# Two experts' rows in one V gather, added in pairs on alternate column halves of TensorE

## What is computed

```python
sc, sel = lax.top_k(cand, PEER_TOPK)
idx = jnp.take_along_axis(cidx, sel, axis=-1)
g = jax.nn.softmax(sc, axis=-1)
u_sel = jnp.take(u_tab, idx, axis=0)
hid = jnp.einsum('td,thkd->thk', xb, u_sel).astype(jnp.float32)
a = (g * jax.nn.gelu(hid, approximate=False)).astype(xb.dtype)
return jnp.einsum('thk,thkd->td', a, jnp.take(v_tab, idx, axis=0))
```

## Time and profile before

| | us |
|---|---|
| median of 3 runs | 3440.01 |
| lowest and highest | 3436.83, 3442.25 |
| profiled execution | 3433.54 |
| its span, first to last instruction | 3431.8 |

### The profile page before, as it was taken

The page is one execution under the profiler, slowest core; times in us unless marked ns, Lnnn a source line. Parts: engine busy times, 40 slices in busy tenths (PEclk is TensorE's granted clock), DMA queues, the critical chain, the costliest instruction groups (busy, mean ns, idle before and its releaser), DMA issues.

```text
span 3431.8 us, 27484 instructions
## 1 busy us (share of the span) xinstructions
PE 2676.2 (78%) x7344; PEld 1233.6 (36%) x7344; DVE 2760.4 (80%) x6506; ACT 797.4 (23%) x1426; POOL 2296.1 (67%) x2198
## 2 busy tenths in 40 slices
PE   7567769988777877877878789988878877666777
PEld 4424424554333323444422234453433323222222
DVE  1588896787899998789898987898899989777761
ACT  4104132662111104142010141663101012200012
POOL 0176666666667777667777677777767767677771
PEclk9788979999889988988999889999988998877788
DMA  6599999999999999999999999999999999999993
GB/s 245 204 392 412 403 354 362 337 317 346 331 330 409 402 410 412 413 403 392 409 409 409 389 402 374 407 367 374 409 374 388 404 408 397 412 393 385 391 401 110
DMA packets 330977, 1277.03 MB, mean 372 GB/s; under 512 B 38148, under 2 KB 39172, under 8 KB 323528
## 3 DMA queue, kind: packets, MB, share of 16 engines
q0 software_dynamic: 313344, 1140.99, 85.8%
q1 hardware_dynamic: 17480, 134.28, 9.8%
HBM read 1267.45 MB, written 6.82 MB: 371 GB/s over the span
## 4 chain that ended last, share of the span: by engine, by line
PE 28%; DVE 25%; DMA 20%; POOL 13%; issue 10%; ACT 3%; DVEq 0%; ACTq 0%; SPq 0%; POOLq 0%
DMA urows<-in_peer_u,idx 14%; DVE urows L1260 9%; PE bank L1512 8%; PE experts L1539 7%; POOL urows L873 6%; POOL vrows L873 6%; DMA vrows<-in_peer_v,idx 4%; PE bank L1522 3%; PE att_out L1512 3%; DVE h L1297 2%; DVE diag L1286 1%; DMA urows<-in_peer_u,idx_sam 1%; DVE work L1156 1%; PE att_out L1522 1%; DVE part L1222 1%
## 5 line engine op out<-in xcount | busy, mean ns | idle before, releaser
L1539 PE MATMUL experts<-vrows,diag 128*128 128x512 f32 (+1 forms) x2876 | 1516.6, 672 | 567.7 <-DVE diag L1286 288.6
L1260 DVE CUSTOM_DVE_ANT_0 urows<-urows,query 128x1024 f32<-128x1024 f32 x1088 | 1311.7, 1211 | 247.2 <-DMA urows<-in_peer_u,idx 211.9
L873 POOL DMA_INDIRECT urows<-in_peer_u,idx x1024 | 1096.8, 1071 | 580.2 <-issue 233.3
L873 POOL DMA_INDIRECT vrows<-in_peer_v,idx x1024 | 1069.2, 1044 | 425.2 <-issue 279.3
L1539 PEld LDWEIGHTS experts<-vrows,diag 128*128 128x128 f32 (+1 forms) x2876 | 555.8, 205 | 1411.5 <-issue 1034.0
L1297 DVE SCALAR_TENSOR_TENSOR h<-vrows,amount,h 128x1024 f32<-128x1024 f32 x369 | 472.6, 1281 | 0.0
L1512 PE MATMUL bank<-weights,xT 128*128 128x512 f32 (+1 forms) x928 | 422.3, 607 | 9.5 <-ACT xT L933 3.7
L1512 PEld LDWEIGHTS bank<-weights,xT 128*128 128x128 f32 (+1 forms) x928 | 161.1, 177 | 247.3 <-issue 236.8
L924 ACT ACTIVATE work<-bank 128x256 f32<-128x256 f32 (+2 forms) x74 | 31.1, 421 | 682.1 <-PE bank L1730 525.5
L1286 DVE TENSOR_TENSOR diag<-ident,amount 128x512 f32<-128x512 f32 x256 | 175.8, 687 | 2.4 <-DVE amount L1270 0.3
L1512 PE MATMUL att_out<-weights,xT 128*128 128x512 f32 (+1 forms) x352 | 163.2, 614 | 0.0
(11 more groups left out here) (189 smaller groups left out, 2456.6 us busy)
## 6 DMA issues: line engine op xcount, KB each, us to landing
weights<-in_w_in SPq DMA_DIRECT2D x25, 2048.0 KB, 10.5
weights<-in_w_out SPq DMA_DIRECT2D x10, 2048.0 KB, 10.4
weights<-in_w_peer_q SPq DMA_DIRECT2D x10, 2048.0 KB, 10.4
urows<-in_peer_u,idx POOLq DMA_INDIRECT x1024, 9.8
vrows<-in_peer_v,idx POOLq DMA_INDIRECT x1024, 9.8
weights<-in_w_ple_gate SPq DMA_DIRECT2D x8, 2048.0 KB, 10.5
weights<-in_w_ple SPq DMA_DIRECT2D x4, 1024.0 KB, 8.1
weights<-in_sub_keysT SPq DMA_DIRECT2D x5, 512.0 KB, 6.7
```

Source lines behind the costliest of these rows:

```text
L873: pool.indirect_dma_start(out=rows[:, where, :], out_offset=None, in_=table, in_offset=bass.IndirectOffsetOnAxis(ap=index, axis=0))\
L1260: dve.tensor_tensor_reduce(row, row, query[:, :], 1.0, 0.0, ALU.mult, ALU.add, hid[:, j % 2, k:k + 1]).then_inc(dotted.sem, 1)
L1539: last = pe.matmul(experts[c][0:ROWS[t], :], diag[:, (4 * j + q) % ND, k % QUARTER, 0:ROWS[t]], vrows[:, n % NV, 512 * c:512 * c + 512], s ...
```

## The change

The gather of a column of `v` brought one expert's row for each of the tile's 128 tokens. Now column c brings the rows of two experts for one half of the tokens: partitions 0 to 63 hold expert 2i and partitions 64 to 127 expert 2i+1, for the tokens of half x, where c = 2i+x. For that the indices are written a second time, folded, into `idx_v` (`fold`: four instructions of 64 partitions and 8 columns), and the amounts are written folded in the first place, by four instructions instead of one. The gathers stay as many and as large.

The matrix that PE holds for a column is 128x64, made from `folded`, two identities one above the other: it adds the two experts of each of 64 tokens at once. Column 2i goes to partitions 0 to 63 of the `experts` banks, column 2i+1 to partitions 64 to 127, so to the two column halves of the array. Both columns of a pair are added at the odd step, bank by bank, the halves in turn. The sample tile has its 32-column matrices as before, but every second row goes to partitions 64 to 95, and `add_experts` adds both parts. DVE adds no row any more; `shares` and `adder` are gone.

```diff
+HALF = P // 2
...
-DVE_ROWS = [(), (2,), (1, 2), (0, 1, 2)]
...
-def adder(j, k):
-    return "dve" if k % QUARTER in DVE_ROWS[SHARES[j, k // QUARTER]] else "pe"
...
+        folded = sb("folded", [P, HALF])
...
+        idx_v = sb("idx_v", [P, SAMPLE, H * TOPK], U32)
...
-        diag = sb("diag", [P, ND, QUARTER, P])
+        diag = sb("diag", [P, ND, QUARTER, HALF])
...
+        added = Signal(sem("added"), steps)
...
+                if b < 2:
+                    select(folded[:, :], [[-1, HALF]], ALU.not_equal, 1.0, base=-HALF * b)
...
+            def folded_column(j, s):
+                _, t, e = ITEMS[j]
+                c = e * TOPK + s
+                return idx_sam[:, c:c + 1] if t == SAMPLE else idx_v[:, t, c:c + 1]
...
-                            pool.wait_ge(*added[adder(*before)].after(before))
-                        gather(i["peer_v"], vrows, n % NV, column(j - 1, k), v_in)
+                            pool.wait_ge(*added.after(before))
+                        gather(i["peer_v"], vrows, n % NV, folded_column(j - 1, k), v_in)
...
+            def fold(out, write):
+                for src in range(2):
+                    for dst in range(2):
+                        at = slice(HALF * src, HALF * src + HALF)
+                        last = write(out[HALF * dst:HALF * dst + HALF, src::2], at, slice(dst, None, 2))
+                        if (src, dst) != (1, 1):
+                            mark(last)
+                return last
...
-                    dve.tensor_tensor(idx[0:r, t, at], part[0:r, 0, :], part[0:r, 1, :], ALU.add)\
-                        .then_inc(routed.sem, 1)
+                    last = dve.tensor_tensor(idx[0:r, t, at], part[0:r, 0, :], part[0:r, 1, :], ALU.add)
+                    if t != SAMPLE:
+                        mark(last)
+                        last = fold(idx_v[:, t, at], lambda out, rows, cols: dve.tensor_tensor(
+                            out, part[rows, 0, cols], part[rows, 1, cols], ALU.add))
+                    last.then_inc(routed.sem, 1)
...
-                dve.tensor_tensor(amount[:, j % 2, :], act_hid[:, j % 2, :],
-                                  gate_sam[:, at] if t == SAMPLE else gate[:, t, at], ALU.mult)\
-                    .then_inc(amounts_done.sem, 1)
+                if t == SAMPLE:
+                    last = dve.tensor_tensor(amount[:, j % 2, :], act_hid[:, j % 2, :], gate_sam[:, at], ALU.mult)
+                else:
+                    shares = gate[:, t, at]
+                    last = fold(amount[:, j % 2, :], lambda out, rows, cols: dve.tensor_tensor(
+                        out, act_hid[rows, j % 2, cols], shares[rows, cols], ALU.mult))
+                last.then_inc(amounts_done.sem, 1)
...
-                    dve.wait_ge(*added["pe"].after(steps[QUARTER * (m - ND + 1) - 1]))
-                full = [P, QUARTER, ROWS[t]]
-                where = spread if t == SAMPLE else ident
-                dve.tensor_tensor(diag[:, m % ND, :, 0:ROWS[t]], where[:, :].unsqueeze(1).to_broadcast(full),
+                    dve.wait_ge(*added.after(steps[QUARTER * (m - ND + 1) - 1]))
+                wide = DEC if t == SAMPLE else HALF
+                full = [P, QUARTER, wide]
+                where = spread if t == SAMPLE else folded
+                dve.tensor_tensor(diag[:, m % ND, :, 0:wide], where[:, :].unsqueeze(1).to_broadcast(full),
                                   amount[:, j % 2, QUARTER * q:QUARTER * q + QUARTER].unsqueeze(2).to_broadcast(full),
                                   ALU.mult).then_inc(diag_made.sem, 1)
...
-            def add_row(j, k):
+            def add_experts(j):
                 t = ITEMS[j][1]
-                n = j * TOPK + k
-                dve.wait_ge(v_in[n % NV], 16 * (n // NV + 1))
-                if added["dve"].count[j, k] > 1:
-                    dve.wait_ge(added["dve"].sem, added["dve"].count[j, k] - 1)
-                dve.scalar_tensor_tensor(out=h[:, t, :], in0=vrows[:, n % NV, :], scalar=amount[:, j % 2, k:k + 1],
-                                         in1=h[:, t, :], op0=ALU.mult, op1=ALU.add).then_inc(added["dve"].sem, 1)
...
+                dve.wait_ge(*added.after((j, TOPK - 1)))
+                groups = (0, HALF) if t == SAMPLE else (0,)
+                for lo in groups:
+                    if lo:
+                        settle()
+                    for c in range(2):
+                        x = h[0:ROWS[t], t, 512 * c:512 * c + 512]
+                        last = dve.tensor_tensor(x, x, experts[c][lo:lo + ROWS[t], :], ALU.add)
+                        if (lo, c) != (groups[-1], 1):
+                            mark(last)
...
-            def add_rows(j, k):
+            def add_pair(j, k):
...
+                for x in range(n, n + 2):
+                    pe.wait_ge(v_in[x % NV], 16 * (x // NV + 1))
                 first = e == 0 and k == 0
-                final = e == items_in_tile(t) - 1 and k == TOPK - 1
+                final = e == items_in_tile(t) - 1 and k == TOPK - 2
+                wide = DEC if t == SAMPLE else HALF
                 for c in range(2):
-                    last = pe.matmul(experts[c][0:ROWS[t], :], diag[:, (4 * j + q) % ND, k % QUARTER, 0:ROWS[t]],
-                                     vrows[:, n % NV, 512 * c:512 * c + 512], start=first, stop=final)
-                last.then_inc(added["pe"].sem, 1)
+                    for x in range(2):
+                        last = pe.matmul(experts[c][HALF * x:HALF * x + wide, :],
+                                         diag[:, (4 * j + q) % ND, k % QUARTER + x, 0:wide],
+                                         vrows[:, (n + x) % NV, 512 * c:512 * c + 512], start=first, stop=final)
+                        if c:
+                            last.then_inc(added.sem, 1)
...
-                    for k in {0: [], 1: [0, 1]}.get(k, [k]):
-                        if 0 < j <= ITEM_COUNT and adder(j - 1, k) == "pe":
-                            add_rows(j - 1, k)
+                    if k % 2 and 0 < j <= ITEM_COUNT:
+                        add_pair(j - 1, k - 1)
```

More of the change, by code:

```diff
@@ L523 @@
 GATE_NUMBER = {s: n for n, s in enumerate(GATES)}
-DVE_ROWS = [(), (2,), (1, 2), (0, 1, 2)]
-PE_ROW = 1.75
-DVE_ROW = 0.43
-DVE_STEP = 1.0
-WINDOW = 5
-def shares():
-    at = [n for n, s in enumerate(SCHEDULE) if s[0] == "peer"]
-    between = [[sum(load(s)[e] for s in SCHEDULE[a:b]) for e in range(2)]
-               for a, b in zip(at, at[1:] + [len(SCHEDULE)])]
-    out = {}
-    for j in range(ITEM_COUNT):
-        for q in range(4):
-            if ITEMS[j][1] == SAMPLE:
-                out[j, q] = 0
-                continue
-            here = (j + 1) * TOPK + QUARTER * q + 2
-            near = between[max(0, here - WINDOW):here + WINDOW]
-            pe, dve = (QUARTER * sum(x[e] for x in near) / len(near) for e in range(2))
-            most = len(DVE_ROWS) - (ITEMS[j][2] == 0 and q == 0)
-            out[j, q] = min(range(most),
-                            key=lambda n: max(pe + PE_ROW * (QUARTER - n), dve + DVE_STEP * QUARTER + DVE_ROW * n))
-    return out
-SHARES = shares()
-def adder(j, k):
-    return "dve" if k % QUARTER in DVE_ROWS[SHARES[j, k // QUARTER]] else "pe"
 def encoder(nc, i, o):
@@ L705, in encoder @@
         diag_made = Signal(sem("diag_made"), [(j, q) for j in range(ITEM_COUNT) for q in range(4)])
-        added = {who: Signal(sem(f"added_by_{who}"), [x for x in steps if adder(*x) == who])
-                 for who in ("pe", "dve")}
+        added = Signal(sem("added"), steps)
         tiles_in_order = [(l, t) for l, t, e in ITEMS if e == 0]
@@ L854, in _ @@
             chain = [0]
-            for buf, value in ((ident, 0.0), (spread, 0.0), (neg_tri, -1.0), (neg_ones, -1.0),
+            for buf, value in ((ident, 0.0), (spread, 0.0), (folded, 0.0), (neg_tri, -1.0), (neg_ones, -1.0),
                                (mask, 0.0), (ones_row, 1.0), (eps_col, EPS)):
@@ L1287, in make_diag @@
+                where = spread if t == SAMPLE else folded
+                dve.tensor_tensor(diag[:, m % ND, :, 0:wide], where[:, :].unsqueeze(1).to_broadcast(full),
                                   amount[:, j % 2, QUARTER * q:QUARTER * q + QUARTER].unsqueeze(2).to_broadcast(full),
                                   ALU.mult).then_inc(diag_made.sem, 1)
-            def add_row(j, k):
-                t = ITEMS[j][1]
-                n = j * TOPK + k
-                dve.wait_ge(v_in[n % NV], 16 * (n // NV + 1))
-                if added["dve"].count[j, k] > 1:
-                    dve.wait_ge(added["dve"].sem, added["dve"].count[j, k] - 1)
-                dve.scalar_tensor_tensor(out=h[:, t, :], in0=vrows[:, n % NV, :], scalar=amount[:, j % 2, k:k + 1],
-                                         in1=h[:, t, :], op0=ALU.mult, op1=ALU.add).then_inc(added["dve"].sem, 1)
@@ L1300, in add_experts @@
             def add_experts(j):
                 t = ITEMS[j][1]
```

(12 more changed lines are left out.)

1 line of the change is left out of this document (removed).

## The result

The changed kernel takes 3515.68 us (median of 4 runs, 3514.85 to 3517.0) against 3441.13 us for the kernel before on the same chip: a ratio of 1.0219, 95% interval 1.0203 to 1.0235. It is 2.2% slower, where the forecast was 1% faster. The profiled execution has a span of 3513.3 us.

A forecast was written before the change was run, and what follows sets the result against it. Bounds differ by window (transfers at a 412 GB/s ceiling, PE, DVE, POOL's issue); gains and losses, 0 - 22 - 5 + 8 + 16 + 11 + 15 + 15, sum to 38 us won: 3440 - 38 = 3402, rounded to 3400 us, range 3335 to 3600.

The forecast's parts named there:

- The price of a pair: On PE, two rows added on overlapping column halves: 1.72 us a pair, plus 0.29 us for the change of width.
- The choice on which I had said that the sum turned: Taking 0.86 us a row on PE (column halves overlap, chance 0.65) rather than 1.72 (no overlap).
- the pricing of PE by windows of 300 us: PE's busy time per window, less old rows at 1.72 us, plus all rows at 1.0 us, held against the window's length.
- 343-600 and 1800-2100: Windows where PE's sum hardly changes and POOL is less delayed: two thirds of the shortfall won, 16 and 11 us.
- the 40 that I had named as a sign of being wrong: Prediction wrong if pairs overlap and the two full windows, 600-900 and 2100-2400, still stretch by over 40 us.
- the rivals: No overlap: about 3665 us, chance 0.21; half an overlap: 3475 to 3480, 0.14; PE no bound: 3330 to 3350, within full overlap.
- the range given for full overlap: 3340 to 3450 us for the whole kernel if the column halves run at the same time, chance 0.65.
- The threshold: From about 1.15 us a row on PE, the loss in the two full windows exceeds the other gains.
- the chances for the slower side: Chance that the kernel gets slower: 0.65*0.07 + 0.11 + 0.21, given as 0.35.
- 3000-3300 and the tail: Undelayed POOL gathers win 15 us in 3000-3300; cheaper rows on PE after the last gathers win 15 us.
- The later release of buffers: V buffers of even rows come free a step (some 3 us) later; 100 us at most, taken as nothing.
- the rule on loads that the prediction quoted: Weight loads on PE overlap matmuls only where the row group differs; both halves share it, so loads would be exposed.

The follow-up runs named there:

- two_on_dve: The kernel before, with DVE given at most two of a quarter's four rows, never three, and PE adding the others one by one; 3517.71 us, ratio 1.0224.
- by_quarter: The changed kernel with the old scheme kept in the 89 quarters with three rows on DVE, pairs everywhere else; 3411.03 us, ratio 0.9913.
- fold_on_act: by_quarter with the folding of indices and gates moved from DVE to ACT, an item ahead, and the gelu written folded; 3394.43 us, ratio 0.9873.
- the two kernels with idle rows: The changed kernel with 369 added DVE instructions that change nothing computed: both inputs in SBUF, 3545.42 us (1.031); one in PSUM, 3543.51 us (1.0293).
- late_none: The kernel before, with no rows on DVE from item 58 on; PE adds them at full width, one by one; 3430.74 us, ratio 0.9973.
- pair_wait: The kernel before, with PE's rows added only at the odd step, after the gathers of both steps; 3438.01 us, ratio 0.9992.
- seven_v: The changed kernel with seven V buffers instead of eight; 3534.09 us, ratio 1.0274.

## Why the prediction was wrong

- **The price of a pair was right**: 1.87 us and 0.19 us on the neighbour, against 1.72 and 0.29. The choice on which I had said that the sum turned was made rightly, with 0.65 of the chance on it, and the sum still came out with the wrong sign.
- **The step that failed is the pricing of PE by windows of 300 us, in which the full pieces vanish.** In 600-900 I found 291 of 300 us and wrote 0. In 343-600 and 1800-2100 I wrote that PE's sum hardly changes, which holds for the whole windows, and counted gains of 16 and 11 us. But each of them holds a piece in which PE had no room: 515-600 with 83.5 of 85 us busy and 5 rows on PE, 1987-2038 with 51 of 51 and 4 rows. In such a piece nothing absorbs added work: in items 8-12, 25 us more of rows and 27 us more of time. `two_on_dve` shows that PE's added rows alone make 73 of the 86 us that the stretches lost, and `by_quarter` that the loss goes when those rows go back to DVE. What makes the other 13 us is not separated.

  The work of each window, followed into the changed kernel by the number of `u` gathers begun, took this much more (less is won):

  | window before | forecast, us | measured, us |
  |---|---|---|
  | 0-343 | 0 | +8 |
  | 343-600 | -16 | +18 |
  | 600-900 | 0 | +14 |
  | 900-1200 | +5 | +5 |
  | 1200-1800 | 0 | +2 |
  | 1800-2100 | -11 | +24 |
  | 2100-2400 | +22 | +23 |
  | 2400-2700 | -8 | +9 |
  | 2700-3000 | 0 | +2 |
  | 3000-3300 | -15 | -16 |
  | 3300 to the end | -15 | -7 |

  So 2100-2400, where the whole window was full and the sum said so, was right to a microsecond, and the two full windows together stretched by 37 us, just under the 40 that I had named as a sign of being wrong. 343-600 and 1800-2100 alone are 69 of the 120 us between forecast and measurement. The time lies within the whole range of 3335 to 3600 only because that left room for the rivals; the range given for full overlap, 3340 to 3450, was missed.
- **The threshold was wrong with it.** I let the slower side begin at 1.15 us a row; at a measured 1.03 the kernel was already 75 us slower. In a full stretch the old scheme's PE price was 1.72 us for a quarter, and two pairs cost 4.1. Only below 0.43 us a row would pairs have broken even there.
- **DVE's relief was not a gain where PE or the folding took its place.** Items 0-8 lost 12 us: DVE, busy for 82% and 92% of their two halves before, has the folding on top, and `fold_on_act` wins 12 us there against `by_quarter` by taking it off. DVE's relief was worth something, 28 to 30 us over the run by the two kernels with idle rows, and is contained in the result; POOL's shows no worth outside the end, by these two against each other.
- **Two slips.** The sentence that the windows not shown stand at 402 GB/s or more holds for 1200-1800 and 2700-3000, not for 0-343, which stands at 313 (373 from the first gather, at 130, on) and whose work lost 8 us. And the chances for the slower side add up to 0.37, not 0.35.
- **The end was right in mechanism and nearly in size**: 15 + 15 us forecast for 3000-3300 and the tail, 16 + 7 measured. POOL's gather fell to 0.957 us as forecast (`late_none` and the sums above are in line with it, though no run turned that one cause on and off).
- **The small terms were right**: the diagonal 423 ns (424), the folding 165 ns (170), DVE busy 2336 us (2300). The line of the pairs was busy 1348 us, not about 1000: 1375 of its 4352 instructions took 1.06 us instead of 0.59, all of them while the granted clock stood at its lower level (1.2 GHz). They lie where PE has room; items 8-12 and 40-44 have only 18 and 5 of them among 264 each. The later release of buffers, taken at nothing, was right for the pair's wait as far as `pair_wait` tries it (0.9992), while `seven_v` gives a buffer some 18 us.

## What to carry to other kernels

A change that moves work to an engine must be priced stretch by stretch at that engine's busiest, cut as finely as the work changes character: there the loss is the work added less the idle time left, whatever the average says. A scheme chosen by load (here three rows of four on DVE where PE is full) and a cheaper instruction are not rivals: keep the choice, and use the cheaper form where the choice leaves room. And a large wait (POOL for PE, 505 us) may be the shadow of a full engine: taking a buffer away made the wait longer and the full stretches no longer.

## What the runs showed of the hardware

Two matmuls in 32-bit floats on the two column halves of the array (128x64 each, 512 columns) run at the same time: 8 instructions in 1.87 us against 3.58 us on one half. Their weight loads do not stand in the way, although both halves use the same 128 rows; the rule on loads that the prediction quoted from the Trainium skill ("TensorE: Matmul & The Clock Gate", "The mechanism") would have exposed them, though the same section excepts loads into the background weight buffer, and the measurement decides. Pairs back to back cost less than pairs one by one (3.58 us for two against 2*1.87). A DVE instruction of 128x1024 delays POOL's indirect gathers when both its inputs lie in SBUF (1044 ns a gather on average) and not when one lies in PSUM (953 ns), at the same duration on DVE (1219 and 1216 ns).
